# Seven half-width products per weight slab (Strassen's scheme) in an encoder trunk, and a reordered last norm

## Chip, cores and metric

One core of one Trainium2 chip runs the whole program in one launch. The metric is the device time of that core in microseconds; lower is better. Everything is computed in float32.

## The reference, cut to what matters

The model is one layer over 256 frames of width 1024, written here as one would write it by hand:

```
h    = rmsnorm(x);  proj = h @ w_in        # 1024 -> xa, ya, uv, z, xbc, dt, three gates of 1024
y_A  = rglru(xa, ya) @ w_a_proj            # gated linear recurrence
y_B  = sgu(uv)       @ w_b_proj            # spatial gating
y_C  = ssd(z, xbc, dt) @ w_c_proj          # chunked state space scan, then a grouped rmsnorm
x    = x + (sig(gA)*y_A + sig(gB)*y_B + sig(gC)*y_C) @ w_out
x    = x + attention(rmsnorm(x) @ w_q, rmsnorm(mem) @ w_kv) @ w_o      # 4 heads over 256 memory rows
x    = x + moe(rmsnorm(x))                 # 32 experts, each frame in two of them
out  = rmsnorm(x)
```

Each dense weight is 1024 by 1024 or a 1024-column part of a wider one; each expert has 1024x1024 and 512x1024 weights.

## The kernel before, in words

**Layout.** Activations are kept transposed: a tensor such as hT is 128 partitions x (8 feature tiles x 256 frames). Weights come from HBM in **slabs** of 512 output columns (128 partitions x 8 input tiles x 512 columns, 2048 KB). There are 36 slabs, listed in SLABS (L105 to L116) in the order of use. They pass through three slots of the tile `ring`; a slab is loaded as soon as the slab three before it has been used (`slab`, L361).

**Dense work.** Two units make one slab. `dense` (L1216) computes one: 2 output tiles x 8 input tiles, each a matmul with a 128x128 piece of weights as the stationary operand and 256 frames as the moving one. The profile has two matmul instructions and two weight loads for each of these float32 matmuls, so a slab is 64 matmul records. All dense calls share line L1225. A unit takes one of 8 PSUM banks in turn (BANK, L93), and `begin` (L1199) waits until the bank's earlier user has been read.

**Order around the change.** TensorE's order is written out by hand in `order` (L70 to L89) and in the tensor block: after the last scan heads (y7) come the branches A, B, C through `branch` (L1383): two gate units, two projection units, twice. Then w_out (wo), the keys (k) with the norm's sum (xn) in their middle, the queries (q), scores (sc), values (va), attention, w_o (ao), the router, and the 32 experts. ScalarE evaluates each gate unit with a Sigmoid (`gates`, L627, through `evac`, L560). VectorE multiplies it with the projection (`merge`, L935; lines L942, L945, L947), adds the w_out result to x (`add_x`, L980) and computes the norms (L954, L956, L986, L988). GpSimd does a few sums: one product of the third branch (L444), one pairwise sum for its norm (L448), and the sums of squares for the norms of x (L452 to L468).

**Expert weights.** Each expert has three 2048 KB parts (`part`, L369, issued at L375 by SyncE), which go through eleven slots: six of `ring`, `params`, and four of `blk`. SyncE's queue issues four parts early, while TensorE is in the projection pC, and the others as their slots come free (L387 to L401). From the first expert on, part k waits for the use of part k-11. The last part is split into four (L407).

**Last norm.** After the last scatter (L1509), TensorE closes the sums (L1577) and spreads the final gain over the partitions (L1581); ScalarE squares both row tiles (L727) and takes a root (L731); VectorE copies the gain (L1182), takes the reciprocal (L1184) and multiplies four pieces (L1188), each of which SyncE stores (L420).

## Time and profile before

| what | value |
|---|---|
| time, median of 3 runs | 1019.6 us (1018.25 to 1019.66) |
| the profiled execution's own time | 1017.95 us |
| its span, first to last instruction | 1016.1 us |
| TensorE busy (matmul) | 868.5 us, 85% |
| TensorE weight load busy | 634.0 us, 62% |
| VectorE, ScalarE, GpSimd busy | 244.5, 192.1, 17.8 us |
| HBM read | 283.08 MB |

In the profile, PE is TensorE's matmuls and PEld its weight loads, DVE is VectorE, ACT ScalarE, POOL GpSimd, SP SyncE. The page shows the span in 40 slices of 25.4 us: a digit is the busy share in tenths, PEclk the granted TensorE clock in tenths of full. A row of a group gives line, engine, operation, output and inputs, shapes and count; then busy time in us, the mean of one in ns; then the idle time before them and what ended it. A row of the timeline gives start and duration in us, and the number of instructions in it. Matmuls are pipelined, so their mean duration (380 ns) is longer than the distance from one to the next.

### The profile page before, as it was taken

To read this page: it belongs to the slowest core of one execution; us is meant where nothing else is said; L and a number is where in the kernel's file an instruction comes from. 1 tells how busy PE (TensorE), PEld (TensorE's weight loads), DVE (VectorE), ACT (ScalarE), POOL (GpSimd) and SP (SyncE) were. 2 spreads that over 40 slices of the span, in tenths; PEclk is the share of its full clock that TensorE was granted. 3 is DMA by queue.
4 is the path that set the end of the run, shared out by engine and by line. 5 is a ranking of instruction groups with operands and counts; after the bars stand their busy time and mean duration, and the time that the engine had idled before them with its cause. 6 is when DMAs were issued, how large, how long until landed. Compare 5 with 4: busy or idle time off the path is not lost.

```text
span 1016.1 us, 15322 instructions
## 1 busy us (share of the span) xinstructions
PE 868.5 (85%) x6808; PEld 634.0 (62%) x6808; DVE 244.5 (24%) x654; ACT 192.1 (19%) x347; POOL 17.8 (2%) x25
## 2 busy tenths in 40 slices
PE   9999999999999999999999999666766666666574
PEld 8888856888888888888658655333333333333332
DVE  2353001734041211020210534212211211221222
ACT  2322146741012000010220212111011111101112
POOL 1000000002000000010001000000000000000000
PEclk9999999999999999999999999979888997988988
DMA  8733533524344468444455599999999999999994
GB/s 297 240 138 131 189 130 139 181 90 156 129 171 166 166 268 335 142 166 165 166 208 206 221 426 426 428 426 427 427 428 426 428 426 428 426 426 426 428 425 198
DMA packets 62391, 285.12 MB, mean 281 GB/s; under 512 B 6692, under 2 KB 11640, under 8 KB 50168
## 3 DMA queue, kind: packets, MB, share of 16 engines
q1 hardware_dynamic: 52736, 278.96, 68.8%
q10 hardware_dynamic: 9592, 5.19, 1.9%
q8 instruction: 55, 0.90, 0.4%
q14 instruction: 8, 0.07, 0.0%
HBM read 283.08 MB, written 1.06 MB: 280 GB/s over the span
## 4 chain that ended last, share of the span: by engine, by line
PE 65%; DMA 23%; SPq 5%; another core or an unknown queue 2%; DVE 2%; issue 1%; ACT 1%; DVEq 0%
PE bank L1225 42%; DMA ring<-in_w_gate_up_dram 10%; DMA blk<-in_w_down_dram 8%; PE bank L1237 5%; PE bank L1533 5%; DMA blk<-in_w_gate_up_dram 5%; SPq L375 4%; PE bank L1553 3%; SPq L407 2%; PE bank L1298 1%; PE bank L1517 1%; PE bank L1509 1%; PE bank L1421 1%; PE bank L1441 1%
## 5 line engine op out<-in xcount | busy, mean ns | idle before, releaser
L1225 PE MATMUL bank<-blk,ring 128*128 128x256 f32 x1984 | 432.4, 380 | 2.4 <-DVE blk L947 1.5
L1225 PEld LDWEIGHTS bank<-blk,ring 128*128 128x128 f32 x1984 | 375.8, 190 | 55.3 <-DVE blk L947 1.9
L1533 PE MATMUL bank<-ring,cbm 128*32 128x256 f32 x1088 | 78.9, 438 | 45.1 <-DMA ring<-in_w_gate_up_dram 44.8
L1533 PEld LDWEIGHTS bank<-ring,cbm 128*32 128x32 f32 x1088 | 39.1, 123 | 79.7 <-issue 55.6
L1533 PE MATMUL bank<-blk,cbm 128*32 128x256 f32 x768 | 53.8, 427 | 30.8 <-DMA blk<-in_w_gate_up_dram 30.8
L1097 DVE TENSOR_TENSOR cbm<-bank,gq 128x256 f32<-128x256 f32 x33 | 14.0, 424 | 259.1 <-PE bank L1517 259.1
L1533 PEld LDWEIGHTS bank<-blk,cbm 128*32 128x32 f32 x768 | 28.0, 119 | 51.3 <-issue 32.2
L1553 PE MATMUL bank<-ring,cbm 128*32 128x256 f32 x576 | 38.3, 408 | 24.9 <-DMA ring<-in_w_down_dram 23.8
L1237 PE MATMUL bank<-ring,blk 128*128 128x512 f32 x128 | 55.8, 592 | 0.0
L706 ACT ACTIVATE cbm<-bank 128x128 f32<-128x128 f32 x32 | 8.9, 277 | 242.4 <-PE bank L1533 242.4
L560 ACT ACTIVATE blk<-bank 128x512 f32<-128x512 f32 x28 | 16.7, 597 | 168.7 <-PE bank L1225 168.6
L1553 PE MATMUL bank<-blk,cbm 128*32 128x256 f32 x352 | 29.4, 489 | 19.8 <-DMA blk<-in_w_down_dram 19.5
L1553 PEld LDWEIGHTS bank<-ring,cbm 128*32 128x32 f32 x576 | 18.8, 115 | 42.1 <-DMA ring<-in_w_down_dram 29.0
L1517 PE MATMUL bank<-blk,dec 128*32 128x256 f32 x528 | 42.3, 436 | 1.9 <-DVE dec L1082 1.9
L1237 PEld LDWEIGHTS bank<-ring,blk 128*128 128x128 f32 x128 | 24.3, 190 | 28.4 <-issue 28.2
L1509 PE MATMUL bank<-cbm,dec 32*128 32x256 f32 x528 | 37.8, 400 | 0.5 <-ACT cbm L709 0.5
L709 ACT COPY cbm<-bank 128x256 f32<-128x256 f32 x32 | 11.9, 372 | 139.0 <-PE bank L1553 139.0
L1517 PEld LDWEIGHTS bank<-blk,dec 128*32 128x32 f32 x528 | 24.1, 130 | 15.8 <-issue 8.6
L1553 PEld LDWEIGHTS bank<-blk,cbm 128*32 128x32 f32 x352 | 12.7, 132 | 33.4 <-DMA blk<-in_w_down_dram 23.6
L1509 PEld LDWEIGHTS bank<-cbm,dec 32*128 32x128 f32 x528 | 23.9, 184 | 14.8 <-issue 13.2
L790 DVE SCALAR_TENSOR_TENSOR ring<-bank,first,ring 128x255 f32<-128x255 f32 (+2 forms) x48 | 20.7, 476 | 30.1 <-ACT ring L517 29.5
L945 DVE TENSOR_TENSOR blk<-blk,bank 128x512 f32<-128x512 f32 x8 | 5.5, 686 | 87.1 <-PE bank L1225 87.1
(274 smaller groups left out, 615.0 us busy)
## 6 DMA issues: line engine op xcount, KB each, us to landing
ring<-in_w_gate_up_dram SPq DMA_DIRECT2D x34, 2048.0 KB, 49.8
blk<-in_w_gate_up_dram SPq DMA_DIRECT2D x24, 2048.0 KB, 50.2
ring<-in_w_in_dram SPq DMA_DIRECT2D x19, 2048.0 KB, 7.7
ring<-in_w_down_dram SPq DMA_DIRECT2D x18, 2048.0 KB, 50.3
blk<-in_w_down_dram SPq DMA_DIRECT2D x10, 2048.0 KB, 50.3
params<-in_w_gate_up_dram SPq DMA_DIRECT2D x6, 2048.0 KB, 50.0
ring<-in_w_kv_dram SPq DMA_DIRECT2D x4, 2048.0 KB, 8.2
params<-in_w_down_dram SPq DMA_DIRECT2D x3, 2048.0 KB, 51.3
```

What stands on the lines that cost most here:

```text
L375: sp.dma_start(slot(s).rearrange("p (k n) -> p k n", k=4), src).then_inc(filled[s], 16)
L407: sp.dma_start(slot(TURNS[k % RING])[:, r * D:(r + 1) * D], w_down[0, NE - 1].rearrange("(p k) n -> p k n", p=P)[:, r, :]).then_inc(row_fi ...
L560: a.activation(dst[:, i:i + 2, :], halves(ps), func, scale=scale).then_inc(read[family(name)], 1)
L709: a.copy(yS, down_bank[:, 0:COLS]).then_inc(sem["yS_ready"], 1)
L790: last = v.scalar_tensor_tensor(out=acc(f0 + f)[:, j:], in0=ps[:, f * T:(f + 1) * T - j], scalar=col(w, (CONV - 1 - j) * tiles_ + f0 + f), ...
L1097: v.tensor_tensor(xeN, gu_bank(p)[:, T:2 * T], gq[:, :], ALU.mult).then_inc(sem["xn3_ready"], 1)
L1225: last = mm(ps[:, f * T:(f + 1) * T], w[:, k, c:c + P], src[:, k, :], start=k == 0, stop=k == KD - 1)
L1237: last = mm(ps[:, :], src[:, k, t * P:(t + 1) * P], w[:, k, :], start=k == 0, stop=k == KD - 1)
L1509: mm(x3_bank[q][:, t * COLS:(t + 1) * COLS], scat[q * WIN:(q + 1) * WIN, p, t * P:(t + 1) * P], yS[q * WIN:(q + 1) * WIN, :], start=False, ...
L1517: last = mm(gu_bank(p)[q * WIN:(q + 1) * WIN, T:2 * T], hot[:, t], x2N[:, t, q * COLS:(q + 1) * COLS], start=t == 0, stop=t == NT - 1)
L1533: last = mm(gu_bank(p)[c * WIN:(c + 1) * WIN, 0:2 * SEG], xe[:, xin, 4 * j + k, :], w[:, k, :, c, :], start=4 * j + k == 0, stop=4 * j + k ...
L1553: last = mm(down_bank[q * WIN:(q + 1) * WIN, 0:COLS], hmT[:, k * WIN:(k + 1) * WIN], w[:, k, q * COLS:(q + 1) * COLS], start=k == 0, stop= ...
```

## The change

For 17 slabs (all gate and projection slabs except the first gate slab of A, and those of w_out, keys and queries) the two units are replaced by `strassen`: the slab is cut into four quarters of 512 inputs x 256 outputs, the activations into four quarters of 512 features x 128 frames, and seven products of quarters are computed in place of eight. Each product is 2 x 4 matmuls with 128 moving columns. GpSimd forms four combinations of the weight quarters for each slab (`combine`), VectorE four combinations of the activation quarters for each activation tensor (`combos`). ScalarE copies three of the products out of PSUM (`mids`), VectorE adds up the results (`sums`, `fold`, `merge`, `onto_x`). The buffers for them lie in the three ring slots that held the early expert parts, so SyncE issues those four parts after the queries. Some small work moves: the sum of squares of x from GpSimd to VectorE, the scale of the queries into the softmax. In the last norm the gain is spread and multiplied in earlier, the squares are taken in four pieces, and the value that tells of overflow experts is read before the last scatter.

```diff
@@ order of units
+    def seven(name, h):
+        j = SEVEN[name, h] = len(SEVEN)
+        return [f"x{j}"] + [f"s{3 * j + r}" for r in range(3)]
     for b in "ABC":
-        for h in (0, 2):
-            order += [f"g{b}{h}", f"g{b}{h + 1}", f"p{b}{h}", f"p{b}{h + 1}"]
+        for h in range(2):
+            order += [f"g{b}0", f"g{b}1"] if (b, h) == ("A", 0) else seven("g" + b, h)
+            order += seven("p" + b, h)
...
@@ sync
-            early = SLAB_OF["wo1"]
-            for n in range(1, early):
+            for n in range(1, NSLAB - 1):
                 slab(n)
-            sp.wait_ge(sem["unit_done"], U["pC0"] + 1)
+            sp.wait_ge(read["s"], 3 * len(SEVEN))
             for k in range(4):
                 part(k // PARTS, k % PARTS, TURNS[k])
...
@@ gpsimd
+            def combine(name, h):
...
+                w11, w12, w21, w22 = (w[:, 4 * k:4 * k + 4, i * T:(i + 1) * T] for i in range(2) for k in range(2))
+                pool.wait_ge(filled[n % PRE], slab_fill(n))
...
+                    pool.wait_ge(sem["product"], 6 * (j - 1) + 2)
+                g.tensor_tensor(out=S1, in0=w21, in1=w22, op=ALU.add).then_inc(sem["weights_ready"], 1)
+                pool.wait_ge(sem["weights_ready"], 4 * j + 1)
+                g.tensor_tensor(out=w21, in0=w11, in1=w21, op=ALU.subtract).then_inc(sem["weights_ready"], 1)
+                if j:
+                    pool.wait_ge(sem["product"], 6 * (j - 1) + 4)
+                g.tensor_tensor(out=S2, in0=S1, in1=w11, op=ALU.subtract).then_inc(sem["weights_ready"], 1)
...
+                    pool.wait_ge(sem["product"], 6 * (j - 1) + 6)
+                pool.wait_ge(sem["weights_ready"], 4 * j + 3)
+                g.tensor_tensor(out=S4, in0=w12, in1=S2, op=ALU.subtract).then_inc(sem["weights_ready"], 1)
+            combine("pA", 0)
             pool.wait_ge(read["y"], KD)
             pool.wait_ge(read["z"], 4)
             g.tensor_tensor(out=ycT, in0=ycT, in1=zT, op=ALU.mult).then_inc(sem["yz_ready"], 1)
...
@@ scalar
+            def mids(name, h):
...
+                act.wait_ge(sem["product"], 6 * j + 2)
+                a.copy(mids_[:, 0:2 * T], bank(f"x{j}")).then_inc(read["x"], 1)
+                act.wait_ge(sem["product"], 6 * j + 4)
+                a.copy(mids_[:, 2 * T:3 * T], bank(f"s{3 * j}")[:, 0:T]).then_inc(sem["mid_copied"], 1)
...
@@ vector
+            def combos(x, t_):
...
+                v.tensor_tensor(t_[:, 0], x12, x11, ALU.subtract).then_inc(sem["combos_ready"], 1)
+                v.tensor_tensor(t_[:, 1], x22, x12, ALU.subtract).then_inc(sem["combos_ready"], 1)
+                dve.wait_ge(sem["combos_ready"], 4 * n + 1)
+                v.tensor_tensor(t_[:, 2], x22, t_[:, 0], ALU.subtract).then_inc(sem["combos_ready"], 1)
+                dve.wait_ge(sem["combos_ready"], 4 * n + 3)
+                v.tensor_tensor(t_[:, 3], x21, t_[:, 2], ALU.subtract).then_inc(sem["combos_ready"], 1)
+            def sums(j):
+                dve.wait_ge(sem["mid_copied"], j + 1)
+                v.tensor_tensor(mid_u, mid_a, part_of(j, 0, 1), ALU.add).then_inc(read["s"], 1)
+                dve.wait_ge(read["s"], 3 * j + 1)
+                v.tensor_tensor(mid_c, mid_u, mid_c, ALU.add)
+                link(v.tensor_tensor(mid_u, mid_u, mid_d, ALU.add))
...
+            def fold(name, h, out, f0):
...
+                sums(j)
+                v.tensor_tensor(quarter_of(out, f0, 1, 1), mid_c, mid_d, ALU.add)
+                dve.wait_ge(sem["product"], 6 * j + 6)
+                v.tensor_tensor(quarter_of(out, f0, 0, 0), mid_a, part_of(j, 1, 0), ALU.add)
+                v.tensor_tensor(quarter_of(out, f0, 0, 1), mid_c, part_of(j, 1, 1), ALU.add).then_inc(read["s"], 1)
+                take(f"s{3 * j + 2}")
+                v.tensor_tensor(quarter_of(out, f0, 1, 0), mid_u, part_of(j, 2, 0), ALU.add).then_inc(read["s"], 1)
...
@@ vector, order of the work
+            combos(xaT, TB)
+            combos(hT, TA)
+            dve.wait_ge(sem["yz_ready"], 1)
+            merge("A", 0)
+            fold("gA", 1, gateT, 4)
+            merge("A", 1)
...
@@ tensor
+            def strassen(name, h, x, t_, made):
...
+                banks_ = [begin(u) for u in (f"x{j}", f"s{3 * j}", f"s{3 * j + 1}", f"s{3 * j + 2}")]
+                def product(i, wt, xt):
+                    ps = banks_[i // 2][:, i % 2 * T:(i % 2 + 1) * T]
+                    for f in range(2):
+                        for k in range(4):
+                            last = mm(ps[:, f * P:(f + 1) * P], wt[:, k, f * P:(f + 1) * P], xt[:, k, :],
+                                      start=k == 0, stop=k == 3)
+                    return last
+                product(0, w11, x11).then_inc(sem["product"], 1)
+                pe.wait_ge(sem["weights_ready"], 4 * j + 1)
+                pe.wait_ge(sem["combos_ready"], 4 * made + 1)
+                product(1, S1, t_[:, 0]).then_inc(sem["product"], 1)
...
+                product(6, w22, t_[:, 3]).then_inc(sem["unit_done"], 4)
...
             for e in range(NE):
                 expert(e)
-            scatter(NE - 1, 1)
             pe.wait_ge(sem["ov_ready"], 1)
             n_ov = pe.value_load(ov_i[0:1, 0:1], min_val=0, max_val=NOV)
+            scatter(NE - 1, 1)
```

The new `merge` has the same steps as `fold`, but each quarter goes to a staging tile, is multiplied by its gate quarter and, for B and C, added to the sum: 15 VectorE instructions for B and C, 11 for A. `onto_x` adds the same sums to x in 11 instructions.

## Rows read from the trace of the kernel before

**Rows 1.** The page: busy time by engine, and lines of the forty slices

```profile
PE 868.5 (85%) x6808; PEld 634.0 (62%) x6808; DVE 244.5 (24%) x654; ACT 192.1 (19%) x347; POOL 17.8 (2%) x25
...
PE   9999999999999999999999999666766666666574
...
PEclk9999999999999999999999999979888997988988
...
GB/s 297 240 138 131 189 130 139 181 90 156 129 171 166 166 268 335 142 166 165 166 208 206 221 426 426 428 426 427 427 428 426 428 426 428 426 426 426 428 425 198
```

**Rows 2.** Groups of instructions by line and shape, TensorE: dense, then scores

```profile
L1225 PE MATMUL bank<-blk,ring 128*128 128x256 f32 x1984 | 432.4, 380 | 2.4 <-DVE blk L947 1.5 <-DVE blk L1007 0.9
...
L1421 PE MATMUL bank<-blk 128*128 128x256 f32 x32 | 7.2, 382 | 0.7 <-ACT blk L560 0.7
```

**Rows 3.** Timeline of TensorE's matmuls (start us, us, what)

```profile
229.00 3.84 PE L1378 MATMUL bank<-params,blk 128*128 128x128 f32 x32
232.77 0.66 PE L1357 MATMUL bank<-dec,ring 128*64 128x256 f32 x4
...
290.65 55.42 PE L1225 MATMUL bank<-blk,ring 128*128 128x256 f32 x256
345.90 1.91 PE L1246 MATMUL bank<-ident,blk 128*128 128x128 f32 x16
347.65 55.42 PE L1225 MATMUL bank<-blk,ring 128*128 128x256 f32 x256
```

**Rows 4.** Timeline of TensorE's weight loads

```profile
25.74 3.65 PEld L1311 LDWEIGHTS bank<-cbm,blk 128*128 128x128 f32 x32
...
229.00 3.65 PEld L1378 LDWEIGHTS bank<-params,blk 128*128 128x128 f32 x32 [0.17 <-issue]
```

**Rows 5.** Groups of instructions, GpSimd

```profile
L448 POOL TENSOR_TENSOR ring<-ring 128x1024 f32<-128x1024 f32 x1 | 2.3, 2349 | 11.4 <-ACT ring L638 11.4
```

**Rows 6.** Groups of instructions, VectorE and ScalarE

```profile
L1097 DVE TENSOR_TENSOR cbm<-bank,gq 128x256 f32<-128x256 f32 x33 | 14.0, 424 | 259.1 <-PE bank L1517 259.1
...
L954 DVE RECIPROCAL dec<-dec 128x1024 f32<-128x1024 f32 x1 | 6.6, 6553 | 1.8 <-ACT dec L642 1.8
...
L947 DVE TENSOR_TENSOR blk<-blk 128x512 f32<-128x512 f32 x8 | 5.5, 691 | 0.3
...
L709 ACT COPY cbm<-bank 128x256 f32<-128x256 f32 x32 | 11.9, 372 | 139.0 <-PE bank L1553 139.0
...
L681 ACT COPY blk<-bank 128x512 f32<-128x512 f32 x4 | 2.3, 585 | 23.3 <-PE bank L1237 23.3
```

**Rows 7.** Timeline of SyncE's queue: expert parts and a slab

```profile
368.57 1.61 SPq L375 DMA_DIRECT2D ring<-in_w_gate_up_dram  x2
...
488.18 0.37 SPq L365 DMA_DIRECT2D ring<-in_w_o_dram  x1
...
579.33 0.33 SPq L375 DMA_DIRECT2D ring<-in_w_down_dram  x1
```

**Rows 8.** Timeline of all engines, the end of the span

```profile
1005.06 1.15 PE L1509 MATMUL bank<-cbm,dec 32*128 32x256 f32 x16 [0.49 <-ACT cbm L709]
...
1007.56 0.39 PE L1577 MATMUL bank<-zeros 1*128 1x512 bf16 x4 [1.35 <-issue]
...
1008.09 1.02 ACT L727 ACTIVATE ring<-bank 128x1024 f32<-128x1024 f32 x1 [0.86 <-PE bank L1577]
...
1010.84 2.73 DVE L1188 SCALAR_TENSOR_TENSOR ring<-bank,stat,ring 128x512 f32<-128x512 f32 x4
1011.61 2.31 SPq L420 DMA_DIRECT2D out_dram<-ring  x4
```

**Rows 9.** Timeline: the one GpSimd instruction with VectorE work beside it

```profile
234.27 4.53 POOL L444 TENSOR_TENSOR blk<-blk,ring 128x2048 f32<-128x2048 f32 x1 [230.30 <-DVE blk L868]
...
235.01 0.69 DVE L925 TENSOR_TENSOR blk<-blk,bank 128x512 f32<-128x512 f32 x1
235.62 0.88 DVE L922 SCALAR_TENSOR_TENSOR bank<-bank,first,params 128x256 f32<-128x256 f32 x2
```

More of the change, by code:

```diff
@@ L85, in encoder_kernel @@
             order += [f"mt{i}" for i in range(4)]
-    order += [f"wo{i}" for i in range(4)] + ["k0", "k1", "xn0", "k2", "k3"]
-    order += [f"q{i}" for i in range(4)] + [f"sc{i}" for i in range(4)] + [f"va{i}" for i in range(4)]
+    order += seven("wo", 0) + seven("wo", 1) + seven("k", 0) + ["xn0"] + seven("k", 1)
+    order += seven("q", 0) + seven("q", 1) + [f"sc{i}" for i in range(4)] + [f"va{i}" for i in range(4)]
     order += ["pt0", "pt1", "o0", "pt2", "o1", "pt3", "o2", "o3"]
@@ L958, in _ @@
             last.then_inc(sem["yC_ready"], 1)
-            merge(1, 0)
+            merge("B", 0)
+            fold("gB", 1, gateT, 4)
             dve.wait_ge(sem["mem_rms"], 1)
@@ L972, in _ @@
                 last.then_inc(read["mt"], 1)
-            merge(2, 0)
-            merge(2, 1)
+            fold("gC", 0, gateT, 0)
+            merge("C", 0)
+            fold("gC", 1, gateT, 4)
+            merge("C", 1)
+            dve.wait_ge(sem["unit_done"], U[last_of("gC", 1)] + 1)
+            combos(mergedT, TA)
+            dve.wait_ge(sem["unit_done"], U[last_of("pC", 1)] + 1)
+            combos(memT, TB)
             def add_x(name):
@@ L980, in add_x, with onto_x @@
                 v.tensor_tensor(xT[:, s, :], xT[:, s, :], halves(ps), ALU.add).then_inc(read[family(name)], 1)
-            for i in range(4):
-                add_x(f"wo{i}")
+            def onto_x(name, h):
+                j = SEVEN[name, h]
+                f0 = 4 * h
+                x11, x12, x21, x22 = (quarter_of(xT, f0, i, jj) for i in range(2) for jj in range(2))
+                sums(j)
+                v.tensor_tensor(x11, x11, mid_a, ALU.add)
+                v.tensor_tensor(x12, x12, mid_c, ALU.add)
+                v.tensor_tensor(x21, x21, mid_u, ALU.add)
+                link(v.tensor_tensor(x22, x22, mid_c, ALU.add))
+                v.tensor_tensor(x22, x22, mid_d, ALU.add)
+                dve.wait_ge(sem["product"], 6 * j + 6)
+                v.tensor_tensor(x11, x11, part_of(j, 1, 0), ALU.add)
+                v.tensor_tensor(x12, x12, part_of(j, 1, 1), ALU.add).then_inc(read["s"], 1)
+                take(f"s{3 * j + 2}")
+                v.tensor_tensor(x21, x21, part_of(j, 2, 0), ALU.add).then_inc(read["s"], 1)
+            for h in range(2):
+                onto_x("wo", h)
+            dve.wait_ge(sem["x1sq_ready"], 2)
+            for n in (4, 2, 1):
+                last = v.tensor_tensor(x1sq[:, 0:n, :], x1sq[:, 0:n, :], x1sq[:, n:2 * n, :], ALU.add)
+                last.then_inc(sem["x1sum_ready"], 1)
+                if n > 1:
+                    dve.wait_ge(sem["x1sum_ready"], 1 if n == 4 else 2)
+            fold("k", 0, KT, 0)
             dve.wait_ge(read["xn"], 1)
@@ L987, in _ @@
             for f in range(KD):
-                v.scalar_tensor_tensor(out=hxT[:, f, :], in0=xT[:, f, :], scalar=col("gxa", f), in1=x1rms,
-                                       op0=ALU.mult, op1=ALU.mult).then_inc(sem["hx_ready"], 1)
+                last = v.scalar_tensor_tensor(out=hxT[:, f, :], in0=xT[:, f, :], scalar=col("gxa", f), in1=x1rms,
+                                              op0=ALU.mult, op1=ALU.mult)
+            last.then_inc(sem["hx_ready"], 1)
+            dve.wait_ge(sem["hx_ready"], 1)
+            dve.wait_ge(sem["unit_done"], U[last_of("wo", 1)] + 1)
+            combos(hxT, TA)
+            fold("k", 1, KT, 4)
+            for h in range(2):
+                fold("q", h, QT, 4 * h)
             for h in range(XA_HEADS + 1):
@@ L1392, in _ @@
+            for i in range(2):
+                dense(f"gA{i}", hT)
+            pe.wait_ge(sem["yA_ready"], 1)
+            strassen("pA", 0, xaT, TB, 0)
+            strassen("gA", 1, hT, TA, 1)
+            strassen("pA", 1, xaT, TB, 0)
             pe.wait_ge(sem["csum_ready"], 1)
@@ L1395, in _ @@
                 end(mm(ps[:, :], onesm[:], csq[:, 4 * i:4 * i + 4:2, :], start=True, stop=True))
-            branch("B", uT, read["sg"], SGU_G)
+            pe.wait_ge(read["sg"], SGU_G)
+            for h in range(2):
+                strassen("gB", h, hT, TA, 1)
+                strassen("pB", h, uT, TB, 2)
             pe.wait_ge(sem["memn_ready"], NT)
@@ L1536, in ffn @@
                     if j == 0:
-                        if behind:
+                        if behind and not rows:
                             gather(n + 1, 1 - p)
-                        pe.wait_ge(sem["placed_ready"], n + 1 + (xin != p))
+                        pe.wait_ge(sem["placed_ready"], n + 1)
                         pe.wait_ge(sem["scat_ready"], n + 1)
@@ L1579, in _ @@
                    start=False, stop=True).then_inc(sem["x3_done"], 1)
-            for q in range(NQ):
-                last = mm(psum[q][:, 0:COLS], ones[q * WIN:q * WIN + 1, :], gfq[q * WIN:q * WIN + 1, :],
-                          start=True, stop=True)
-            last.then_inc(sem["gfin_spread"], 1)
 _INS = ['x', 'mem', 'norm_mix', 'w_in', 'conv_a_w', 'conv_a_b', 'lru_gx_w', 'lru_gx_b', 'lru_ga_w',
```

337 lines of the change are left out of this document (225 added, 112 removed).

## The prediction

> **What bounds the kernel now.** The page comes first [rows 1]. TensorE is busy nine tenths or more in the first 23 slices while HBM moves 90 to 335 GB/s; from slice 24 the GB/s stand at 426 to 428, and two slices later TensorE falls to six or seven tenths. So there are two stages: until about 580 us matmuls bind, afterwards the stream of expert weights does. A microsecond saved before 580 us starts the same transfers a microsecond earlier and so comes off the end. Then the groups by line [rows 2]: the dense line has 1984 matmuls with only 2.4 us of idle time in front of them, 1.5 of it at w_out, and the scores waited 0.7 us. The dense stage is one unbroken stream, whose price is the distance from one matmul to the next. That comes from the timeline [rows 3]: 256 dense matmuls start at 290.65 and what follows starts at 345.90, so four slabs take 55.25 us, one 13.81 us, one matmul record 215.8 ns.
>
> **TensorE, the main term.** Seven products of 8 matmuls are 56, in the profile 112 records of 128 moving columns, in place of 64 of 256. If columns alone counted, seven eighths of 13.81 would be 12.09 us. But with 128 columns the weight load can become the longer part. The nearest row is the spatial gating at L1378: the same 128x128 weights, 128 columns, 32 records. Its loads take 3.65 us from first start to last end [rows 4]; less the last one's own 0.19 (the group's 192 ns), 31 distances are 3.46 us, 111.6 ns each. The loads of L1311, with only 16 moving columns, take the same 3.65 us, so this pace is the loads', not the columns'. A slab becomes 112 x 0.1116 = 12.50 us, 1.31 us less than 13.81, and **17 slabs give 22.3 us**. Bounds: transposes with 128 columns stand 1.75 us for 16, 109.4 ns [rows 3], which gives 12.25 and 26.5 us. From the first L1378 matmul to the next group is 3.77 us for 32, 117.8 ns [rows 3], because that short group also pays a gap in front; with it a slab is 13.19 and the gain 10.5 us. I take 111.6, since strassen's waits are no denser than those of L1378, one for eight records.
>
> **Waits of TensorE at the seams.** At wo the new kernel still waits, but only its second product does. After pC's last product VectorE has three instructions of 0.42 (as the 424 ns of L1097) and the first combination of 0.69 (L947) [rows 6], 2.0 us with their links, against 1.8 us that the first product covers. Some 0.4 us are left of the 1.5: gain 1.1. The scores wait only for q's first half, which is long there: gain 0.7.
>
> **GpSimd.** Four instructions on 128x1024 a slab, 2.35 each [rows 5], are 9.4 us of 12.5. None binds: S1 starts after the second product of the slab before, S4 after its sixth, ends 0.6 us into the slab and is wanted 8.9 us in. Its queue also holds the product at L444 (4.53 us [rows 9]), now behind pA's combinations; it ends about 7 us after yA is ready, and merge A is not wanted before product four, 7 us in. The pairwise sum (2.35) ends 3 us into pA's second slab, and cn wants it at its end. The norm's sums that leave GpSimd cost VectorE some 2.4 us beside the first key slab. All at nothing, covered by TensorE; without that cover each is its own length.
>
> **VectorE and ScalarE.** A fold is 7 instructions of about 0.42, a merge 15: 9.2 us for two slabs of 25. The rest lies in the same gaps: a set of combinations is 4 x 0.69 = 2.8 us, the reciprocal 6.55 [rows 6]. A bank is wanted again two slabs later, so a late fold costs nothing until it is a slab late. For the queries the chain after the first key slab is a root (some 2 us), a reciprocal of a quarter of L954's length (1.7) and eight products of 0.42, together some 7.5 us, beside a key slab of 12.5. ScalarE adds 0.59 and 0.37 a slab [rows 6]. At nothing.
>
> **SyncE.** Four expert parts move from 368.57, beside pC, behind the last query sum, about 488 in the old time [rows 7]. At 427 GB/s a part takes 4.9 us. From there to the first reuse at 579.33 lie 91 us, and thirteen transfers (two slabs of w_o, eleven parts) need 13 x 4.9 = 64. The second slab of w_o, now behind five parts, lands some 34 us in and is wanted at 59. At nothing; if the 27 us of spare were gone, each missing microsecond would count in full, up to 19.6.
>
> **The end** [rows 8]. Before, the closing matmuls wait 1.35 us behind the last scatter for a value to be read; now that read lies beside the copy in front of the scatter, which may wait for it instead: about 0.5 back. From the first square (1008.09) to the last issue (1013.92) are 5.8 us. Now gain products and squares overlap, and only root, reciprocal and scalings of 512 follow: about 2.9 for four squares, 1.0 for root, bias and reciprocal, 1.2 for four issues: 5.1. **Gain 1.2 us**; it lies between nothing and 2.5.
>
> **Sum.** 22.3 + 1.1 + 0.7 + 1.2 = 25.3 us. Against the profiled execution's 1017.95 that is 992.7. That execution is 1.65 under the median of 1019.6; against the median it is **994 us**. With the bounds of pace and end this case spans 989 to 1007.
>
> **Rival one: GpSimd and VectorE get in each other's way in part.** In the old kernel GpSimd is busy for 17.8 us in all [rows 1], in the new one for 160 us more, three quarters of the dense stage. The longest overlap in the trace is L444 beside L925 and L922 [rows 9]: L925 takes its usual 0.69. But these read one operand from PSUM; VectorE instructions with both inputs in SBUF never run beside a GpSimd sum in this trace, and the new kernel has some 146 of them (27 in folds, 58 in merges, 14 at w_out, 28 combinations, 19 in norms). So nothing here speaks for or against it. If each such instruction (0.34 to 0.69) and the GpSimd one beside it only stretch, the folds come late where VectorE already has long work (B's reciprocal, the seams to C, wo, k, q). At 2 to 3 us at each of five seams that is 12 us back: 1006.
>
> **Rival two, slower than before: full exclusion.** Here VectorE waits out a whole GpSimd sum, 2.35 us, before each instruction with two SBUF inputs, as long as GpSimd has the next sum ready. From product two of a slab to the start of the next GpSimd is busy without a gap; VectorE passes one instruction between two sums. A merge with 11 of them, begun 7.6 us into its slab (four products and a copy), gets two through before the slab ends, and six or seven with their links stand between the last sum and the read that frees the bank: some 4 us. Walking the slabs so, TensorE waits 3.4 us in the first pA, 4.0 before the second, 5.1 before B's second projection, 4.5 before C, 5.1 at wo, 3.8 before the keys, 4.1 before the queries: 30 us. 994 + 30 = **1024**. It decides from 25.3 us of such waits on, 1.5 a slab; below that the kernel is still faster. Against it: when TensorE waits, GpSimd does too, and VectorE catches up.
>
> The Trainium skill has this rule on its page "SBUF — State Buffer", section "Who interferes with whom": VectorE with two SBUF inputs and GpSimd reading SBUF share one read interface, and whoever issues first holds it for the whole instruction. By that rule the sum would be rival two's. The overlap in the trace agrees with its other half (one SBUF input doesn't contend); no row shows the half that matters here.
>
> **Rival three: the pace is the worse one.** Waits inside a slab open gaps, and a record costs 117.8 ns: 1006. Break-even of the main term is 13.81/112 = 123.3 ns.
>
> **Chances.** The forecast has 0.46. Rival one has 0.20, rival two 0.20, rival three 0.10; what is left, 0.04, is a stall of another kind (the expert parts too late, a wait for a slab). A measurement of this kernel can tell about 0.2% (2 us) from no change. Faster takes the forecast, rivals one and three and a small part of rival two, whose 30 us may be 20: 0.78. Same: 0.07, from that rival near its break-even. Slower: 0.15. The range runs from 988 (pace 109.4 with all of the end) to 1020 (rival two with little of its excess), which leaves out about 0.05 below and 0.14 above; the likeliest case alone has 989 to 1007.
>
> **What would show it.** In the profile after, the new product line has 1904 matmuls (17 x 112), about 112 ns apart, a slab 12.5 us; loads cover nearly all of their time; TensorE's waits in front of them are under 3 us; SyncE's first reuse of an expert slot is near 555 us (579.33 before [rows 7]); four GpSimd sums a slab stand at 2.35. Rival one or two is right where VectorE's 0.42 instructions or GpSimd's 2.35 become longer, or idle time ends on GpSimd, and TensorE waits for VectorE before pB, gC, wo, k and q. Rival three shows as 118 ns without such waits. The sum as a whole is wrong if the 426 GB/s don't begin with that reuse, so that what is saved before it is lost behind it.

## The result, and the profile after

The change makes the kernel slower by half a percent: 1024.99 us median (1024.56 to 1026.44, 4 runs) against 1019.09 (1018.25 to 1019.66, 4 runs), a ratio of 1.0051 with a 95% interval of [1.0032, 1.0070]. The profiled execution took 1024.79 us, its span is 1023.0. The forecast was 994. What happened is rival two, almost to the microsecond: TensorE got its faster products and stood still for what they had saved.

The page of the kernel after (busy time by engine, then lines of the forty slices), against [rows 1]:

```profile
PE 860.1 (84%) x7608; PEld 648.6 (63%) x7608; DVE 414.2 (40%) x827; ACT 201.5 (20%) x371; POOL 180.7 (18%) x89
...
PE   8999999999799799898999899767666776666575
...
GB/s 295 238 152 130 171 151 116 185 90 158 165 124 165 156 96 169 158 165 127 304 410 228 180 426 426 428 425 426 425 430 427 425 427 426 427 429 426 426 426 192
```

VectorE's busy time has grown by 169.7 us and GpSimd's by 162.9, while some of TensorE's slices fall to seven and eight tenths in the stage where all had nine before. The stream behind it is the same as before: 426 GB/s or a little more.

Groups of instructions by line and shape of the kernel after: first TensorE's products and VectorE's instructions with both inputs in SBUF, then those with one input in a PSUM bank, last a GpSimd sum.

```profile
L1599 PE MATMUL bank<-ring 128*128 128x128 f32 x1088 | 130.5, 279 | 4.8 <-DVE ring L1025 4.8
L1599 PE MATMUL bank<-blk,ring 128*128 128x128 f32 x816 | 101.6, 283 | 15.8 <-DVE ring L1086 12.8 <-DVE blk L1170 3.0
...
L1038 DVE TENSOR_TENSOR ring<-ring 128x256 f32<-128x256 f32 x17 | 30.8, 1809 | 0.0
...
L1074 DVE TENSOR_TENSOR ring<-ring 128x256 f32<-128x256 f32 x6 | 14.8, 2460 | 0.2
...
L1035 DVE TENSOR_TENSOR ring<-ring,bank 128x256 f32<-128x256 f32 x17 | 7.1, 417 | 37.7 <-ACT ring L683 37.6
...
L1086 DVE TENSOR_TENSOR ring<-ring,bank 128x256 f32<-128x256 f32 x6 | 2.5, 414 | 0.1
...
L478 POOL TENSOR_TENSOR ring<-ring 128x1024 f32<-128x1024 f32 x17 | 41.1, 2416 | 296.5 <-PE bank L1561 229.5
```

The names on the right of the arrow decide. An instruction on 128x256 that reads "ring,bank" takes 0.41 to 0.42 us, as before the change. The same size reading "ring" twice takes 1.81 us in the mean and up to 2.57; L1074, which always falls beside GpSimd's sums, took at least 2.457 in each of its six. From 245 to 500 us every wait of TensorE ends on VectorE.

One merge in the timeline of the kernel after (start us, us, engine, line):

```profile
323.13 0.41 DVE L1035 TENSOR_TENSOR ring<-ring,bank 128x256 f32<-128x256 f32 x1
323.45 2.35 POOL L478 TENSOR_TENSOR ring<-ring 128x1024 f32<-128x1024 f32 x1 [2.90 <-PE bank L1599]
323.57 2.51 DVE L1037 TENSOR_TENSOR ring<-ring 128x256 f32<-128x256 f32 x1
325.88 2.41 POOL L480 TENSOR_TENSOR ring<-ring 128x1024 f32<-128x1024 f32 x1
326.01 2.57 DVE L1038 TENSOR_TENSOR ring<-ring 128x256 f32<-128x256 f32 x1
...
328.26 2.53 POOL L483 TENSOR_TENSOR ring<-ring 128x1024 f32<-128x1024 f32 x1
328.62 2.46 DVE L1074 TENSOR_TENSOR ring<-ring 128x256 f32<-128x256 f32 x1
...
331.57 2.45 DVE L1071 TENSOR_TENSOR blk<-blk 128x256 f32<-128x256 f32 x1
...
336.18 0.41 DVE L1086 TENSOR_TENSOR ring<-ring,bank 128x256 f32<-128x256 f32 x1
...
336.74 3.75 PE L1599 MATMUL bank<-blk,ring 128*128 128x128 f32 x16 [4.50 <-DVE ring L1086]
```

Each of the first three blocked VectorE instructions begins 0.1 to 0.4 us behind a GpSimd sum and ends 0.3 us behind that sum's end: 325.88 + 2.41 = 328.29, and VectorE is done at 328.58. It is drawn as a long instruction, not as idle time, so the view of the waits on VectorE shows nothing. Four blocked instructions in this merge make L1086, which frees the bank, late, and TensorE waits 4.50 us for it at the start of pB's second slab. The merge also begins late: its copies stand since 314.78, but the third branch's norm comes first in VectorE's order, with a reciprocal of 6.54 us and eight products that take 6.18 us (3.3 in e1 below, where nothing blocks them).

The granted clock is in the windows. A row gives the window and its length, then the busy time of PE, PEld, DVE, ACT and POOL, then PEclk, the DMA share and GB/s:

```profile
277.60:283.00 5.40, 5.34 (x25) 5.37 (x26) 2.97 (x8) 1.86 (x3) 0.00 (x0) 0.50 0.39 151
283.00:300.00 17.00, 17.00 (x142) 16.05 (x142) 11.57 (x14) 4.20 (x6) 11.11 (x5) 1.00 0.36 125
```

**Where the time went.** TensorE waits at five places for VectorE: 5.12 us before pA's second slab, 4.50 before pB's, 3.17 before C, 4.77 at w_out, 2.96 before the queries, 20.5 us in all. Behind four of the five its granted clock is 0.50 (the 1.2 GHz level in place of 2.4) for some microseconds. The first 64 records after 277.66 take 9.82 us to the next group in place of 64 x 0.1117 = 7.15; the other places lose 2.2 (336.74), 1.5 (413.32, 48 records) and 1.7 us (466.81): 8.0 with the first one's 2.7. From 247.19 to the scores at 493.55 are 246.4 us, where 17 slabs of 12.50 and 3.9 of other matmuls would be 216.4. The 30.0 between them are the 20.5, the 8.0 and 1.4 more. Of these 1.4, 0.8 belong to the waits too: each is counted from the modelled end of the last matmul, 0.17 us behind the point where the next would have started (332.24 and 330.29 + 16 x 0.1117 = 332.08). The last 0.6 stay open. So the scores start 4.7 us later than before (493.55 against 488.84), and SyncE's first reuse is at 585.82 in place of 579.33 [rows 7]; the other 1.8 us come in the router's stage, again at a clock of 0.50 behind a wait of 2.8. The last scatter stands 427.24 us behind that reuse (before, 425.73) and 9.94 us ahead of the end (before, 11.04). 6.5 + 1.5 - 1.1 = 6.9 us is the growth of the span, from 1016.1 to 1023.0.

### The profile page after: what moved, and what is told of

Same layout as the page of the kernel before. It is cut to its first block, busy times and chain, and to the rows that moved or that the text cites. A ratio compares the mean times of both kernels' runs of the same rounds, so it can differ in the third digit from the quotient of the medians.

```text
span 1023.0 us, 17278 instructions
## 1 busy us (share of the span) xinstructions
PE 860.1 (84%) x7608; PEld 648.6 (63%) x7608; DVE 414.2 (40%) x827; ACT 201.5 (20%) x371; POOL 180.7 (18%) x89
## 4 chain that ended last, share of the span: by engine, by line
PE 51%; DMA 24%; DVE 15%; SPq 5%; another core or an unknown queue 2%; issue 1%; ACT 1%; ACTq 0%; DVEq 0%
PE bank L1428 18%; PE bank L1599 11%; DMA ring<-in_w_gate_up_dram 10%; PE bank L1440 5%; PE bank L1780 5%; SPq L399 5%; DMA ring<-in_w_down_dram 5%; DMA params<-in_w_gate_up_dram 5%; DMA blk<-in_w_down_dram 5%; PE bank L1802 3%; DVE ring L1038 2%; PE bank L1501 1%; DVE ring L1074 1%; PE bank L1752 1%
## 5 line engine op out<-in xcount | busy, mean ns | idle before, releaser
L1428 PE MATMUL bank<-blk,ring 128*128 128x256 f32 x896 | 196.9, 380 | 0.8 <-DVE blk L1197 0.8
L1428 PEld LDWEIGHTS bank<-blk,ring 128*128 128x128 f32 x896 | 169.1, 190 | 25.0 <-issue 1.4
L1599 PE MATMUL bank<-ring 128*128 128x128 f32 x1088 | 130.5, 279 | 4.8 <-DVE ring L1025 4.8
L1599 PEld LDWEIGHTS bank<-ring 128*128 128x128 f32 x1088 | 127.8, 196 | 5.0 <-issue 4.9
L1599 PE MATMUL bank<-blk,ring 128*128 128x128 f32 x816 | 101.6, 283 | 15.8 <-DVE ring L1086 12.8
L1599 PEld LDWEIGHTS bank<-blk,ring 128*128 128x128 f32 x816 | 98.4, 199 | 17.1 <-issue 13.8
L478 POOL TENSOR_TENSOR ring<-ring 128x1024 f32<-128x1024 f32 x17 | 41.1, 2416 | 296.5 <-PE bank L1561 229.5
L1780 PE MATMUL bank<-blk,cbm 128*32 128x256 f32 x768 | 58.9, 458 | 33.5 <-DMA blk<-in_w_gate_up_dram 33.4
L1780 PEld LDWEIGHTS bank<-blk,cbm 128*32 128x32 f32 x768 | 29.3, 127 | 57.1 <-issue 38.1
L483 POOL TENSOR_TENSOR ring<-ring 128x1024 f32<-128x1024 f32 x17 | 43.5, 2557 | 0.0
L480 POOL TENSOR_TENSOR ring<-ring 128x1024 f32<-128x1024 f32 x17 | 42.1, 2478 | 1.3
L489 POOL TENSOR_TENSOR ring<-ring 128x1024 f32<-128x1024 f32 x17 | 40.8, 2401 | 6.2 <-DVE blk L1015 3.5
```

What stands on the lines that cost most here:

```text
L478: g.tensor_tensor(out=S1, in0=w21, in1=w22, op=ALU.add).then_inc(sem["weights_ready"], 1)
L480: g.tensor_tensor(out=w21, in0=w11, in1=w21, op=ALU.subtract).then_inc(sem["weights_ready"], 1)
L483: g.tensor_tensor(out=S2, in0=S1, in1=w11, op=ALU.subtract).then_inc(sem["weights_ready"], 1)
L489: g.tensor_tensor(out=S4, in0=w12, in1=S2, op=ALU.subtract).then_inc(sem["weights_ready"], 1)
L1428: last = mm(ps[:, f * T:(f + 1) * T], w[:, k, c:c + P], src[:, k, :], start=k == 0, stop=k == KD - 1)
L1599: last = mm(ps[:, f * P:(f + 1) * P], wt[:, k, f * P:(f + 1) * P], xt[:, k, :], start=k == 0, stop=k == 3)
```

## The experiments

The theory after the result, A: a VectorE instruction with two SBUF inputs and a GpSimd instruction that reads SBUF exclude each other, and the rest follows. Its rivals, B: VectorE simply has too much work (827 instructions in place of 654); C: GpSimd is too slow for its place in the slab.

**e1_write_only.** The same places in the same queue, but GpSimd only writes constants where it summed the weights. Each sum is replaced by three fills in a row (two of 1024 elements a partition and one of 512), which take about as long:

```diff
+            def fill(out):
+
+                for value in (0.03, 0.02):
+                    fill_step[0] += 1
+                    g.memset(out, value).then_inc(sem["fill_step"], 1)
+                    pool.wait_ge(sem["fill_step"], fill_step[0])
+                return g.memset(out[:, 0:2, :], 0.01)
...
-                g.tensor_tensor(out=S1, in0=w21, in1=w22, op=ALU.add).then_inc(sem["weights_ready"], 1)
+                fill(S1).then_inc(sem["weights_ready"], 1)
```

> The changed kernel, but GpSimd only writes constants where it formed its four sums of weight quarters (three fills in a row, together about as long as one sum), so the weight combinations are left out of the computation. GpSimd is as busy as before at the same places, but reads nothing. Theory A, exclusion (a VectorE instruction with two SBUF inputs waits out a GpSimd instruction that reads SBUF): no VectorE instruction of this kind is longer than 0.45 us where it had 2.46, TensorE's waits in the product stage fall from some 20 us to under 2, its half-clock stretches behind them go too, and the time is 993 to 998 us. Rival B, VectorE's own load (its new instructions, their quarter views and links are too slow for the stage by themselves): the same waits before pA, pB, gC, wo and q, and 1020 to 1025 us. Rival C, GpSimd is late: TensorE's waits were for the weight sums; then they would stay, as GpSimd's work is as long as before.

The whole run took 1147.81 us, and that number says nothing of the change: it computes with wrong weight sums, so the experts get other work. Their largest group grew from 1088 to 1728 matmuls, the bytes read from 283 to 346 MB. Up to the values the work is the same, and there the run can be read. Groups of e1 (its L1047, L1048 and L1084 are L1037, L1038 and L1074 of after):

```profile
L1047 DVE TENSOR_TENSOR ring<-ring 128x256 f32<-128x256 f32 x17 | 7.2, 425 | 0.6
...
L1084 DVE TENSOR_TENSOR ring<-ring 128x256 f32<-128x256 f32 x6 | 2.5, 425 | 0.2
...
L471 POOL MEMSET ring<- 128x1024 f32 x136 | 129.5, 952 | 275.7 <-PE bank L1571 231.0 <-PE bank L1609 35.5 <-DVE blk L1025 2.4
...
L1609 PE MATMUL bank<-ring 128*128 128x128 f32 x1088 | 127.1, 275 | 0.9 <-DVE ring L1035 0.9
L1609 PE MATMUL bank<-blk,ring 128*128 128x128 f32 x816 | 96.7, 275 | 0.0
```

GpSimd is about as long busy as in the change (178.4 us and 180.7), VectorE has every one of its instructions of this stage, and these are short again. TensorE waits 0.9 us in 17 slabs. The values' matmuls (L1450) start at 473.29, 27.2 us before those of the change (500.46) and 22.6 before those of the kernel before (495.85). That ends B and C, and it places the loss on what GpSimd reads.

One GpSimd instruction that reads SBUF was left in this stage, the product for the third branch (L504), and it blocks VectorE here too. Timeline of e1:

```profile
247.56 5.06 POOL L504 TENSOR_TENSOR blk<-blk,ring 128x2048 f32<-128x2048 f32 x1
...
248.16 5.01 DVE L1036 TENSOR_TENSOR ring<-blk 128x512 f32<-128x512 f32 x1
```

L1036 is a combination with two inputs in SBUF. It took 5.01 us here, and its median over seven is 0.68.

**e2_half_sums.** Each sum in two instructions of 512 elements a partition:

```diff
-                g.tensor_tensor(out=S1, in0=w21, in1=w22, op=ALU.add).then_inc(sem["weights_ready"], 1)
+                for c in range(2):
+                    c = slice(4 // 2 * c, 4 // 2 * (c + 1))
+                    last = g.tensor_tensor(out=S1[:, c], in0=w21[:, c], in1=w22[:, c], op=ALU.add)
+                last.then_inc(sem["weights_ready"], 1)
```

> The changed kernel with each GpSimd sum in two instructions of 512 elements (1.26 us each in place of one of 2.35), same result. Theory A, exclusion for the length of one GpSimd instruction: a blocked VectorE instruction takes 1.3 to 1.4 us in place of 2.46, VectorE passes twice as many per slab, and TensorE's 30 us of waits and slow clock fall to 5 to 12: 1000 to 1007 us. Rival B, VectorE's own load: no change of the waits, 1025 us. Rival C, GpSimd is late: it is 0.7 us a slab slower now, so 1025 or more.

It took 1017.14 us (1014.86 to 1019.04), 0.9970 [0.9958, 0.9981] of before. Timeline of e2:

```profile
322.13 1.45 POOL L485 TENSOR_TENSOR ring<-ring 128x512 f32<-128x512 f32 x1
322.49 1.37 DVE L1077 TENSOR_TENSOR blk<-blk,ring 128x256 f32<-128x256 f32 x1
```

Groups of the same run:

```profile
L1050 DVE TENSOR_TENSOR ring<-ring 128x256 f32<-128x256 f32 x17 | 22.0, 1297 | 0.0
...
L1611 PE MATMUL bank<-ring 128*128 128x128 f32 x1088 | 130.4, 279 | 4.8 <-DVE ring L1037 4.8
L1611 PE MATMUL bank<-blk,ring 128*128 128x128 f32 x816 | 98.5, 278 | 9.3 <-DVE ring L1098 6.6 <-DVE blk L1182 2.7
```

The length of a blocked VectorE instruction follows the length of the GpSimd instruction in front of it, 1.37 beside 1.45 as it was 2.5 beside 2.4: that is the mark of exclusion. But the sum of TensorE's waits fell only from 20.6 to 14.1 us, and the gain is 8 us, less than was expected; the wait at w_out, 4.8, didn't change. Shorter turns let one VectorE instruction through every 1.4 us, still three times slower than its 0.42.

**e5_psum_operands.** GpSimd keeps all its sums; VectorE reads one operand from PSUM wherever the products or their sums can stay there. 99 of the 146 instructions with two SBUF inputs are gone:

```diff
-                a.copy(mids_[:, 0:2 * T], bank(f"x{j}")).then_inc(read["x"], 1)
-                act.wait_ge(sem["product"], 6 * j + 4)
-                a.copy(mids_[:, 2 * T:3 * T], bank(f"s{3 * j}")[:, 0:T]).then_inc(sem["mid_copied"], 1)
+                a.copy(mids_[:, 0:T], bank(f"x{j}")[:, 0:T]).then_inc(sem["mid_copied"], 1)
...
-                v.tensor_tensor(mid_c, mid_u, mid_c, ALU.add)
-                link(v.tensor_tensor(mid_u, mid_u, mid_d, ALU.add))
+                v.tensor_tensor(mid_c, mid_u, x_part(j, 1), ALU.add).then_inc(read["x"], 1)
+                link(v.tensor_tensor(mid_u, mid_u, part_of(j, 0, 0), ALU.add))
```

The merges do the same: the sum of a quarter is written back to its bank, multiplied by the gate there, and only then added to the merged block. The banks are held longer for it. ScalarE copies one product for each slab in place of three; that it isn't the copies that cost is seen in e1, which has all of them.

> The changed kernel, same seven products and same GpSimd sums, but VectorE takes one operand of each recombination from PSUM in place of a copy in SBUF: two of the three copied products stay in their banks, and the staging tile for merges is the bank itself. Of some 146 VectorE instructions with two SBUF inputs 99 lose one (folds, merges, w_out); left are 28 combinations, 16 norm products, 3 sums. As many VectorE instructions, of the same size. Theory A, exclusion: TensorE no longer waits before pA's second, pB's second, gC and (nearly) wo; the wait before the queries behind the 8 norm products stays at about 3 us with its slow clock; 1001 to 1007 us. Rival B, VectorE's own load or links: no less work for it here, so 1020 to 1025 us. Rival E, a bank is now held until its products are merged: new waits for banks, 1010 or more.

It took **999.55 us** (997.53 to 1002.37, 5 runs) against 1020.86 (11 runs), 0.9800 [0.9779, 0.9821]. Groups of e5:

```profile
L1177 DVE SCALAR_TENSOR_TENSOR blk<-blk,first,dec 128x256 f32<-128x256 f32 x8 | 11.6, 1524 | 0.0
...
L1035 DVE TENSOR_TENSOR ring<-ring,bank 128x256 f32<-128x256 f32 x15 | 6.3, 420 | 0.5
...
L483 POOL TENSOR_TENSOR ring<-ring 128x1024 f32<-128x1024 f32 x17 | 41.3, 2429 | 0.0
...
L1606 PE MATMUL bank<-ring 128*128 128x128 f32 x1088 | 127.3, 275 | 0.9 <-DVE ring L1023 0.9
L1606 PE MATMUL bank<-blk,ring 128*128 128x128 f32 x816 | 96.8, 275 | 1.8 <-DVE blk L1177 1.5 <-DVE blk L1070 0.2
```

The window from 245 to 480 us of e5 (columns as above):

```profile
245.00:480.00 235.00, 232.29 (x1991) 227.88 (x1990) 147.65 (x246) 31.82 (x55) 163.77 (x67) 1.00 0.48 170
```

VectorE and GpSimd are both busy for more than six tenths of that stage and no longer touch each other, except where both inputs are still in SBUF (L1177, the queries' norm, 1.52 in place of 0.48). The granted clock is 1.00 over that window. The time lies below the 1001 to 1007 that were expected, since the wait before the queries is only 1.5 us and no slow clock follows it. The first reuse of an expert slot is at 561.03, 18.3 us before that of the kernel before, and the span (997.4) is 18.7 shorter.

**e6_psum_norms.** e5, with the reciprocals of the branch norm and the queries' norm written to the PSUM banks that their sums of squares came in:

```diff
-            link(v.reciprocal(crms, crms))
+            for i in range(2):
+                last = v.reciprocal(halves(bank(f"cn{i}")), crms[:, 2 * i:2 * i + 2, :])
...
-            link(v.reciprocal(x1rms, x1rms))
+            xrow = bank("xn0")[:, T:2 * T]
+            link(v.reciprocal(xrow, x1rms))
```

> As the kernel with PSUM operands, and the reciprocals of the two norms (third branch, queries) are also written to PSUM, so that their 16 products read one operand from SBUF. Theory A: the last wait, before the queries, goes too, some 3 us with its half-clock stretch 4 to 5; 997 to 1003 us. Left of the gain in the product stage: 17 x 1.31 us less what the 28 combinations still wait. Rival: the wait before the queries was the length of the chain itself (root, reciprocal, eight products); then no change against the kernel before it.

It took 1010.92 us (1008.77 to 1012.26), 0.9900 [0.9884, 0.9916] of before: 11 us worse than e5, which neither of the two cases expected. Timeline of e6:

```profile
289.96 0.69 ACT L699 ACTIVATE dec<-bank,epsc 128x512 f32<-128x512 f32 x1 [0.17 <-PE bank L1639]
...
302.80 6.56 DVE L1106 RECIPROCAL bank<-dec 128x512 f32<-128x512 f32 x2
...
309.40 3.22 DVE L1109 SCALAR_TENSOR_TENSOR blk<-blk,first,bank 128x256 f32<-128x256 f32 x8
...
312.88 2.47 PE L1610 MATMUL bank<-blk,ring 128*128 128x128 f32 x10 [10.46 <-DVE blk L1109]
```

The norm's products are short now (3.22 for eight), and it doesn't matter: in e5 the two banks are free behind the roots, here at 290.65, and now they are held until 312.62. That is 22 us longer: the reciprocal and the products are 9.8 of it, and ahead of them VectorE is at other work. pB's products want those banks. One contended resource was changed for another.

**e7_psum_queries.** Only the queries' half of e6, on top of e5 (the last three lines of the diff above).

> The kernel of e5_psum_operands with one thing more: the reciprocal of the queries' norm is written to the PSUM bank that the sums of squares came in, and the eight norm products read it there, so that they have one operand in SBUF. The branch norm stays as in e5. Theory (e6 lost its time to the bank hold of the branch norm alone, and its queries' part was good): the 1.52 us wait of TensorE ahead of the first query products is gone, no 10 us wait comes near 313 us, and the time is 1 to 2 us under e5: about 998 us, 0.978 of before. Rival (the bank holds of both norms hurt): a new wait of over 1 us at the keys or the queries, and 1000 us or more. Rival 2 (the wait is hidden anyway, since the scores wait for something else): within 0.5 us of e5's 999.6.

**996.48 us** (995.39 to 999.27, 5 runs) against 1019.38 (9 runs), 0.9770 [0.9750, 0.9790]. TensorE's waits before the products are 1.1 us in all, and the first reuse is at 558.66. The values start 2.4 us earlier than in e5 (475.23, 477.62). The wait at the queries is gone, no new one came: the bank hold of the branch norm alone spoiled e6. Against e5 the two intervals overlap, so the run times show no gain of their own. In the profile the products stage is 2.4 us shorter, but the span, 997.5, is not (e5 has 997.4): that execution, the slowest of the five, lost as much in its last expert, see e8.

**e3_last_norm.** The kernel before with the last norm of the change and nothing else: the gain spread into banks during the last expert, no gather behind it, squares beside the products with the gain, scalings of 512 at the end.

```diff
-                    gather(n + 1, xin)
+                    gather(n, xin)
...
+                        if rows:
+                            spread_gfin()
```

> The kernel before with only the end of the change: gain spread and multiplied early, squares in four pieces, the overflow count read before the last scatter. By the two traces the stretch from the last scatter to the end fell from 11.04 to 9.94 us, so this alone should give 1.1 us: 1018.0 against 1019.1. A rival: the early spreading in the last expert costs as much as it saves: 1019.

1021.85 us (1020.05 to 1023.71, 12 runs) against 1019.88 (29 runs), 1.0013 [1.0002, 1.0024]: slower, if by little, where 1.1 us of gain were expected. Timeline of e3:

```profile
995.50 3.64 PE L1582 MATMUL bank<-ring,cbm 128*32 128x256 f32 x32 [3.05 <-DMA ring<-in_w_gate_up_dram]
...
999.69 2.58 PE L1567 MATMUL bank<-gfq,ones 1*128 1x256 f32 x8
1002.20 3.64 PE L1582 MATMUL bank<-blk,cbm 128*32 128x256 f32 x32
1005.77 2.09 PE L1546 MATMUL bank<-cbm,dec 32*128 32x256 f32 x16
...
1010.40 1.15 PE L1546 MATMUL bank<-cbm,dec 32*128 32x256 f32 x16 [0.50 <-ACT cbm L714]
1012.95 0.40 PE L1628 MATMUL bank<-zeros 1*128 1x512 bf16 x4 [1.40 <-issue]
```

A window of the same run:

```profile
995.00:1000.00 5.00, 4.50 (x37) 2.19 (x40) 0.00 (x0) 0.00 (x0) 0.00 (x0) 0.50 0.85 347
```

After the wait for weights (3.05) TensorE is at a clock of 0.50 until about 1007, and 32 records that take 1.93 at full clock take 3.64. In the profile of the kernel before, the last expert's waits were shorter (1.78 and 1.63) and it ran at 1.00 (998.95 to 1005.06). And the wait for a value to be read (1.40) is still in front of the closing matmuls; in the profile of the full change it isn't. So from the last scatter to the end this run has 11.5 us, not the 9.9 of the change, and what the part saves there isn't in it.

**e8_psum_old_last_norm.** e7 with the last norm of the kernel before, so that the same piece is tested from the other side (the diff is that of e3, reversed).

> The kernel of e7 with the last norm put back as it was in the kernel before (the gain spread by four matmuls after the last scatter, the gather one expert ahead with its unused 17th column, the squares and products after them). Theory from e3 (the reordered last norm costs as much as it gives, because without the gather TensorE idles and runs the last expert at half its clock): TensorE's granted clock stays 1.00 in the last expert, last scatter to end is 11 us again in place of 9.9, and the sum is 0 to 2 us faster than e7: about 996 to 998 us. Rival (e3's loss was specific to the kernel before, or noise; the norm is worth the 1.2 us forecast): 999 to 1000 us, 1.2 us slower than e7.

996.88 us (996.46 to 1000.31), 0.9787 [0.9764, 0.9809], beside e7's 0.9770: no difference. The clock part of the expectation held only for the second half of the last expert, and from the last scatter to the end are 10.4 us (9.9 in e7), not 11. Timeline of the last expert in e7:

```profile
974.05 3.64 PE L1788 MATMUL bank<-ring,cbm 128*32 128x256 f32 x32 [3.05 <-DMA ring<-in_w_gate_up_dram]
...
980.75 3.20 PE L1788 MATMUL bank<-blk,cbm 128*32 128x256 f32 x32
```

And in e8:

```profile
972.93 3.64 PE L1739 MATMUL bank<-ring,cbm 128*32 128x256 f32 x32 [3.06 <-DMA ring<-in_w_gate_up_dram]
976.31 1.96 PE L1723 MATMUL bank<-blk,dec 128*32 128x256 f32 x16
...
978.83 1.93 PE L1739 MATMUL bank<-blk,cbm 128*32 128x256 f32 x32
```

And in e5, with the same last norm as e7:

```profile
976.48 3.46 PE L1787 MATMUL bank<-ring,cbm 128*32 128x256 f32 x32 [3.05 <-DMA ring<-in_w_gate_up_dram]
...
980.34 1.53 PE L1772 MATMUL bank<-gfq,ones 1*128 1x256 f32 x8
981.80 1.93 PE L1787 MATMUL bank<-blk,cbm 128*32 128x256 f32 x32
```

All three fall to 0.50 behind a wait of the same length. In e8, with the gather (16 records, 1.96) behind the first 32, the clock is back for the second 32 (1.93). With the gain's eight thin matmuls there it is back in e5 and e9 (1.93), and not in e7 (3.20), e2 and e3 (3.64). So the missing gather doesn't settle it; no run changed the gather alone, and each kernel has one profiled execution. From the first of those records to the end are 21.8 to 22.0 us with the old norm (before, e4, e8); with the new one 20.8 and 20.9 where the clock came back (e9, e5), and 23.5 to 26.4 where it didn't (e7, e2, e3). The reordered norm is worth some 1 us in the first case and costs 1.5 us and more in the second. The change itself has 21.7: its waits there are 1.49 and 1.02, and only its second 32 records are slow (3.04).

**e4_late_parts.** The kernel before with only the move of the four expert parts behind the last query sum.

```diff
-            sp.wait_ge(sem["unit_done"], U["pC0"] + 1)
-            for k in range(4):
-                part(k // PARTS, k % PARTS, TURNS[k])
...
+                    sp.wait_ge(sem["unit_done"], U["q3"] + 1)
+                    for k in range(4):
+                        part(k // PARTS, k % PARTS, TURNS[k])
```

> The kernel before with the four early expert parts issued after the queries, as in the change, and nothing else. Thirteen transfers of 4.9 us then have to fit into the 91 us up to the first reuse of a slot. Theory: they fit, no change, within 1 us of 1019.1. Rival D: the missing head start delays the first experts, part of the 19.6 us of four parts comes back at the end, and the change lost its gain there: 1024 or more.

1019.68 us, 0.9995 [0.9982, 1.0008]: no change.

**e9_psum_half_sums.** e7 and e2 together.

> The kernel of e7 with each GpSimd sum in two instructions of 512 elements a partition, as in e2. Some 47 VectorE instructions with two SBUF operands remain in e7 (the x1 and input combinations, the branch norm). Theory (a blocked VectorE instruction waits out the GpSimd instruction that holds the memory): their durations halve to some 1.4 us, but TensorE waits for under 1 us in all there, so at most 1 us is left to win: 997 to 998.5 us. Rival (GpSimd's doubled count of instructions makes its queue late, its sums then gate the products): TensorE waits on GpSimd by over 1 us, 1000 us or more.

997.47 us (993.82 to 998.98), 0.9772 [0.9748, 0.9796]: the same as e7. With the two engines apart there is nothing left for shorter turns to save.

## Why the prediction was wrong, step by step

- **The main term held.** Where nothing waits, a slab of seven products stands 12.50 us from the next one, in the change (294.56 to 307.06, and on to 319.57) and in e1 (248.72 to 261.22); the pace of 111.6 ns, taken from a group of 32 records, held for whole slabs. Rival three is out. From the first such slab to the scores e1 takes 217.7 us (248.72 to 466.38), the kernel before 241.4 (247.42, one slab behind 233.58, to 488.84). The 23.7 between them are the 22.3 of the main term and 1.3 of waits that fell from 1.50 and 0.69 to 0.93. e1 starts that stage 1.3 us later, so at the values 22.6 are left.
- **The step that failed** is "VectorE and ScalarE ... At nothing". It priced a fold's instructions at 0.42 and a combination at 0.69, from rows in which GpSimd was idle or VectorE had an operand in PSUM. L1037, L1038 and L1074 cost 1.10, 1.81 and 2.46 in their place. The text saw that no row showed such a pair, counted 146 of them, walked the merges by full exclusion and came to 30 us of waits and 1024 us; measured were 30.0 from the first slab to the scores, of which 20.5 are waits and most of the rest is clock, and 1025.0. What was wrong is the step itself, that this work lies in TensorE's shade at its uncontended price, and the weight: 0.20 for full exclusion against 0.46 for a case that needed none, where no row spoke for either. "When TensorE waits, GpSimd does too, and VectorE catches up" spoke against it, and the timeline shows why it is no help: the catching up is the wait.
- The Trainium skill, page "SBUF — State Buffer", section "Who interferes with whom", says that a VectorE instruction with two SBUF inputs contends with a GpSimd instruction that reads SBUF and not with one that only writes it, and that one with a single SBUF input stays clear, outside the two-port modes. All three parts have their number here: 2.46 to 2.57 us beside the sums, 0.42 in e1 beside the constants, 0.42 in e5 with an operand in PSUM. The one reader left in e1 (5.06 us, with a combination of 5.01 beside it) agrees too.
- **The seams** (1.1 + 0.7) were right in kind: in e1 and e5 w_out waits 0.9 us where 1.5 stood, and nothing before the scores. Under the exclusion w_out became the second-worst wait, 4.77.
- **GpSimd at nothing** was right for its own work: no product of weight quarters waits for it in any run, and its sums stretch by 0.1 us in the mean at most (L483, 2.56 in the change beside 2.43 in e5). VectorE paid nearly all of the exclusion.
- **SyncE at nothing** was right: e4, 0.9995 [0.9982, 1.0008], and 426 GB/s in the change.
- **The end** did not come as a gain. 1.1 us were saved behind the last scatter against 1.2 forecast, but the stretch ahead of it grew by 1.5: TensorE ran the second half of the last expert at half clock (32 records in 3.04 us, 16 of the scatter in 1.67 in place of 1.15), which the sum left out. Alone the part costs 0.13% [0.02%, 0.24%], in a run that kept the wait for the read value; with the rest in place (e7 and e8) it can't be told from nothing. In e5 and e9, where the clock came back, it saved some 1 us.
- **What no part priced** is the clock: each wait of 3 us and more was counted at its length, and four of the five in the products stage cost 1.5 to 2.7 us on top. Why the wait of 3.17 before C was not followed by a slow stretch (its 64 records take 7.22), I didn't find out. That the sum still fits rival two's 30 us is luck: of its seven waits two never came (3.4 in the first pA, 3.8 before the keys), and what its waits were too long by, the clock took.
- The chain from the products to the end held: 18.3 us earlier at the first reuse was 18.7 off the span in e5; in e7 20.7 us earlier were 18.6 off, as its last expert ran at half clock. Had VectorE stayed clear of GpSimd, the forecast of 994 would have been near: e7 is at 996.5.

What stays open: 0.6 us of the 30.0, what decides whether the clock is back in the last expert's second half, the router stage's 1.8 us (a slow clock behind a wait of 2.8 us is seen there, the cause of the wait wasn't tried), and a branch norm free of two SBUF inputs that doesn't hold its banks.

## What to carry to other kernels

Before giving GpSimd work beside VectorE, count VectorE's instructions that read SBUF twice: each waits out the GpSimd instruction in front of it if that reads SBUF, so its price is GpSimd's length, 2.5 us here in place of 0.42, and it is drawn as busy time. The cure is not less work but another place for an operand: products left in their PSUM banks turned 1025.0 us into 999.6 (996.5 with the queries' norm, a step that the run times alone don't show), as long as no bank was held past its next use. And a wait on TensorE is worth more than its length where it is followed by a stretch at half clock.

## What the hardware showed that I had not expected

- VectorE bears nearly all of it: its blocked instructions are six times longer (2.5 us in place of 0.42), GpSimd's grow by a twentieth in the mean (2.56 and 2.43).
- In a stage whose granted clock is 1.00 otherwise, it is 0.50 from the first matmul behind waits of 3.0, 4.5, 4.8 and 5.1 us, for up to 5 us (277.60 to 283.00), and not behind one of 3.2. Records at that level stand 0.22 us apart in place of 0.11 (16 in 3.54).
- How soon the clock is back differs between kernels with the same last norm and a wait of the same length: the last expert's second 32 records took 1.93 us in e5 and e9, 3.20 in e7 and 3.64 in e3. With so few executions the cause stays open.
